# Block 2's norms: the shift from two tiles, the order of the sums, who centres, and the order of three FFN products

## The chip, the cores and the metric

One core of a Trainium2 chip runs the whole program. Times are device microseconds of one execution. TensorE multiplies, VectorE (DVE), ScalarE (ACT) and GpSimd (POOL) work elementwise, SyncE (SP) issues the loads.

## The reference, cut to what matters

Two different transformer blocks follow each other, each with two layers, over 512 tokens and 1024 model columns in float32. The change touches block 2 alone. Each of its layers is

```python
mix = hybrid_mixer(x, ...)
x = layer_norm(ALPHA * x + mix, ln1_g, ln1_b)
cross = memory_cross_attention(x, mem, w_mq, w_mkv, w_mo)
x = layer_norm(ALPHA * x + cross, ln2_g, ln2_b)
ff = squared_relu_mlp(x, w_ff1, w_ff2)      # 1024 -> 4096 -> 1024
x = layer_norm(ALPHA * x + ff, ln3_g, ln3_b)

def layer_norm(x, g, b):
    mu = mean(x); var = mean((x - mu) ** 2)
    return (x - mu) * rsqrt(var + 1e-5) * g + b
```

## The kernel before

Activations lie with the model column on the partitions: x is eight chunks of 128 columns by 512 tokens (`x[:, n, :]`). A product's output tile is 128 columns by 512 tokens and is summed over eight chunks of the input. Every float32 operand is split in two parts of a faster format, `hi` and `lo`, and a product takes three matmuls per chunk: w_hi by x_hi (L511), w_lo by x_hi (L514), w_hi by x_lo (L517). `dense` issues the three of one chunk, `tiles` the chunks of one output tile, or of several side by side. Weights come through three staging buffers; ScalarE writes a weight tile's high part (`split_hi`, L998), VectorE its low part (`split_lo`, L1487), into three buffers, so tile n waits for product n - 3. Results go to four PSUM slots in the fixed order of `rings()`.

Each engine has its own written-out program, and semaphores (`did`, `done`) join them; an instruction waits behind everything ahead of it on its engine. `Banks` keeps who must have read a PSUM bank before TensorE writes it again.

A norm follows the eight output tiles of `w_mix`, `w_mo` or the last part of `w_ff2`: six norms in all. Its mean and variance are sums over partitions, so they are matmuls by a matrix of ones, in float32, which take two passes each. So that E[x^2] - mean^2 stays exact, x is first shifted by the mean of its first half of tiles. The steps:

- Tiles 0 to 3: VectorE adds the product to ALPHA x (`added`, L1750); GpSimd adds up the four (`total`, L2209); after product 4, TensorE sums over partitions (`shift_sum`, L864), and ScalarE copies the negative mean (`shift`, L1350).
- VectorE adds the shift to tiles 0 to 3 (`shifted`, L1964); from tile 4 on it adds it to x ahead of the product (`pre`, L1972) and the product after it (`shifted`, L1968). ScalarE squares each shifted tile (L1345), and GpSimd adds up tiles 0 to 6 (`d_sum`, L2216) and their squares (`sq_sum`, L2211 and L2219), 13 operations.
- `tensor_statistics`: four sums, over `total2` (L873), x of tile 7 (L875), the squares (L877) and the last square (L879). ScalarE copies the mean (L1367) and squares it (L1369); VectorE forms the variance (`ln_var`, L2012), ScalarE the reciprocal root (L1041, L1043), VectorE two Newton steps (L1508, L1510).
- `centred` takes the mean off: tiles 0, 2, 3, 6 on VectorE (L2001), 1, 4, 5, 7 on GpSimd (L2226). VectorE multiplies by the root (`ln_scaled`, L2024), ScalarE applies gain and bias twice, to the next product's high part (L1384) and to x (L1385; the last norm writes x alone, L1380), and the low part of even chunks is VectorE's (L2007), of odd chunks GpSimd's (L2231).

Behind `w_mix` TensorE has other work, the keys of the memory (`w_mk`, one tile ahead of the sums and seven after), and then the queries (`w_mq`). Behind `w_mo` come the tiles of `w_ff1`, the first two side by side, behind `w_ff2` of layer 0 the token-major products of the next layer (`token_major`, L562, L564, L568), and behind the last norm the stores of the output.

## Time and profile before

| | before |
|---|---|
| median of three runs | 3048.58 us (3047.69 to 3049.86) |
| profiled execution | 3042.06 us |
| its span | 3040.2 us |
| TensorE busy | 2858.9 us, 94% |
| VectorE, ScalarE, GpSimd busy | 1643.0, 1260.2, 571.0 us |
| mean granted TensorE clock | 0.977 |

The busy times are those of one profiled execution. Matmuls overlap, so the start of one to the start of the next is the time that it holds the engine. A row ends, in brackets, with the idle time of the engine before it and what ended it.

### The profile page before, as it was taken

How to read it: one execution, taken by the hardware profiler on the slowest of the kernel's cores; microseconds unless marked ns; L12 is line 12 of the kernel's file. 1: busy time of each engine (PE TensorE's matmuls, PEld its weight loads, DVE VectorE, ACT ScalarE, POOL GpSimd, SP SyncE). 2: the span in 40 equal slices, each digit the busy share in tenths (PEclk: the TensorE clock that was granted, in tenths of full speed). 3: DMA queues.
4: the chain of work that ended last, by engine and by line, in shares of the span. 5: the costliest groups of instructions: out<-in, count | busy, mean ns of one | idle time of the engine just before them, and what ended most of it. 6: DMA issues, size and time to landing. Idle time of an engine off the chain costs nothing.

```text
span 3040.2 us, 38912 instructions
## 1 busy us (share of the span) xinstructions
PE 2858.9 (94%) x15604; PEld 2371.1 (78%) x15608; DVE 1643.0 (54%) x2509; ACT 1260.2 (41%) x2104; POOL 571.0 (19%) x435
## 2 busy tenths in 40 slices
PE   8988999999979999999999979999799899799997
PEld 7778999998767888886667758888666678588885
DVE  5785644455875744546846353333558664443334
ACT  5673322234763422225445343333344544343333
POOL 2342000011341000002334140000423342400003
PEclk9999999999989999999999989999899999899998
DMA  4111232232112333231133123332211222122221
GB/s 140 45 43 63 91 92 89 91 98 67 44 36 79 98 97 97 86 105 53 60 101 104 45 66 97 97 97 91 72 62 57 94 98 70 56 85 95 97 94 60
DMA packets 71923, 244.35 MB, mean 80 GB/s; under 512 B 9152, under 2 KB 10816, under 8 KB 71744
## 3 DMA queue, kind: packets, MB, share of 16 engines
q1 hardware_dynamic: 66528, 235.50, 24.1%
q10 hardware_dynamic: 5216, 6.36, 0.6%
q8 instruction: 125, 2.05, 0.3%
q14 instruction: 54, 0.44, 0.0%
HBM read 239.73 MB, written 2.10 MB: 80 GB/s over the span
## 4 chain that ended last, share of the span: by engine, by line
PE 78%; DVE 11%; issue 4%; ACT 4%; POOL 3%; DMA 0%; ACTq 0%; DVEq 0%; POOLq 0%
PE psum L511 21%; PE psum L517 21%; PE psum L514 21%; PE psum L536 2%; PE psum L568 2%; PE psum L562 2%; PE psum L564 1%; DVE temp L1915 1%; DVE weights_hi_lo L1487 1%; DVE small L1913 1%; PE psum L914 1%; PE psum L926 1%; ACT weights_hi_lo L998 1%; PE psum L760 1%; POOL temp L2216 1%
## 5 line engine op out<-in xcount | busy, mean ns | idle before, releaser
L511 PE MATMUL psum<-act_hi_lo,weights_hi_lo 128*128 128x512 f32 (+2 forms) x2640 | 822.0, 349 | 17.5 <-ACT act_hi_lo L1384 15.0
L514 PE MATMUL psum<-act_hi_lo,weights_hi_lo 128*128 128x512 f32 (+2 forms) x2640 | 798.0, 340 | 1.9 <-DVE weights_hi_lo L1487 1.9
L517 PE MATMUL psum<-act_hi_lo,weights_hi_lo 128*128 128x512 f32 (+2 forms) x2640 | 796.6, 339 | 0.3
L1487 DVE TENSOR_TENSOR weights_hi_lo<-weights_float,weights_hi_lo 128x1024 fp32r<-128x1024 f32 (+2 forms) x446 | 572.0, 1283 | 263.5 <-ACT weights_hi_lo L998 262.1
L998 ACT ACTIVATE weights_hi_lo<-weights_float 128x1024 fp32r<-128x1024 f32 (+2 forms) x446 | 463.7, 1041 | 507.8 <-PE psum L517 435.3
L511 PEld LDWEIGHTS psum<-act_hi_lo,weights_hi_lo 128*128 128x128 f32 x2640 | 461.2, 190 | 83.2 <-issue 25.2
L511 PE MATMUL psum<-hidden_hi_lo,weights_hi_lo 128*128 128x512 f32 (+1 forms) x1488 | 501.3, 363 | 12.0 <-ACT hidden_hi_lo L1168 7.3
L517 PEld LDWEIGHTS psum<-act_hi_lo,weights_hi_lo 128*128 128x128 f32 x2640 | 458.5, 189 | 58.8 <-DVE act_hi_lo L2007 1.7
L514 PEld LDWEIGHTS psum<-act_hi_lo,weights_hi_lo 128*128 128x128 f32 x2640 | 459.5, 190 | 57.1 <-issue 3.1
L517 PE MATMUL psum<-hidden_hi_lo,weights_hi_lo 128*128 128x512 f32 (+1 forms) x1488 | 493.1, 358 | 1.7 <-POOL hidden_hi_lo L1744 1.2
L514 PE MATMUL psum<-hidden_hi_lo,weights_hi_lo 128*128 128x512 f32 (+1 forms) x1488 | 492.5, 357 | 0.6 <-DVE weights_hi_lo L1487 0.6
L511 PEld LDWEIGHTS psum<-hidden_hi_lo,weights_hi_lo 128*128 128x128 f32 x1488 | 265.4, 189 | 53.9 <-ACT hidden_hi_lo L1168 8.8
L517 PEld LDWEIGHTS psum<-hidden_hi_lo,weights_hi_lo 128*128 128x128 f32 x1488 | 264.7, 189 | 44.0 <-POOL hidden_hi_lo L1744 2.2
L514 PEld LDWEIGHTS psum<-hidden_hi_lo,weights_hi_lo 128*128 128x128 f32 x1488 | 265.3, 189 | 41.2 <-DVE weights_hi_lo L1487 1.5
L1750 DVE SCALAR_TENSOR_TENSOR x_residual<-x_residual,psum 128x512 f32<-128x512 f32 (+1 forms) x136 | 94.0, 691 | 335.1 <-PE psum L517 335.0
L2071 DVE TENSOR_TENSOR hidden_hi_lo<-temp,hidden_hi_lo 128x512 fp32r<-128x512 f32 x64 | 44.3, 692 | 220.9 <-ACT hidden_hi_lo L1454 220.9
L2176 POOL TENSOR_SCALAR temp<-temp,small 128x512 f32<-128x512 f32 (+3 forms) x96 | 106.4, 1119 | 229.1 <-DVE small L1873 229.1
L2209 POOL TENSOR_TENSOR temp<-x_residual 128x512 f32<-128x512 f32 x6 | 13.3, 2216 | 718.6 <-DVE x_residual L1750 718.6
L2112 POOL TENSOR_TENSOR temp<-temp 128x528 f32<-128x528 f32 (+1 forms) x24 | 34.0, 1417 | 434.4 <-ACT temp L1035 433.7
L1202 ACT ACTIVATE hidden_hi_lo<-temp 128x528 fp32r<-128x528 f32 (+1 forms) x44 | 28.1, 639 | 205.3 <-DVE temp L1786 205.3
L1448 ACT ACTIVATE temp<-psum 128x512 f32<-128x512 f32 x64 | 38.2, 598 | 171.9 <-PE psum L517 171.9
L562 PE MATMUL psum<-weights_hi_lo,act_hi_lo 128*128 128x512 f32 (+1 forms) x208 | 84.6, 407 | 20.9 <-ACT weights_hi_lo L998 9.8
(246 smaller groups left out, 3304.3 us busy)
## 6 DMA issues: line engine op xcount, KB each, us to landing
weights_float<-in_w_ff SPq DMA_DIRECT2D x128, 512.0 KB, 3.5
weights_float<-in_w_gu SPq DMA_DIRECT2D x88, 512.0 KB, 3.4
weights_float<-in_w_in SPq DMA_DIRECT2D x70, 512.0 KB, 3.4
weights_float<-in_w_down SPq DMA_DIRECT2D x32, 448.0 KB, 3.3
weights_float<-in_w_out SPq DMA_DIRECT2D x16, 512.0 KB, 3.4
weights_float<-in_w_down SPq DMA_DIRECT2D x16, 512.0 KB, 3.5
weights_float<-in_w_mv SPq DMA_DIRECT2D x16, 512.0 KB, 3.2
weights_float<-in_w_mix SPq DMA_DIRECT2D x16, 512.0 KB, 3.2
```

Of the source, the lines that this page charges most:

```text
L511: e.matmul(slot[:, place:place + c1 - c0], w_hi[:, col], x_hi[:, c0:c1], start=first, stop=False)
L514: e.matmul(slot[:, place:place + c1 - c0], w_lo[:, col], x_hi[:, c0:c1], start=False, stop=False)
L517: mm = e.matmul(slot[:, place:place + c1 - c0], w_hi[:, col], x_lo[:, c0:c1], start=False, stop=final)
L536: mm = e.matmul(slot[:, place:place + c1 - c0], weights, moving[:, c0:c1], start=first, stop=final)
L562: e.matmul(bank, act[:, 0, here], w_hi[:, wk], start=k == 0, stop=False)
L568: mm = e.matmul(bank, act[:, 1, here], w_hi[:, wk], start=False, stop=k == DC - 1)
L998: e.activation(K.parts(n)[0][:, 0:cols], K.staged(n)[:, 0:cols], ACT.Copy).then_inc(*K.did("hi", n))
L1448: e.activation(tmp, K.bank[2 * RING["w_ff1", l, f]], ACT.Relu).then_inc(*did("relu", l, f))
L1487: e.tensor_tensor(lo[:, 0:cols], K.staged(n)[:, 0:cols], hi[:, 0:cols].bitcast(F32), ALU.subtract).then_inc(*K.did("lo", n))
L1750: e.scalar_tensor_tensor(along(x, width), along(x, width), alpha, across(K.psum[slot], width), ALU.mult, ALU.add).then_inc(*K.did(*mark))
L2071: e.tensor_tensor(lo, K.relu[f % 3][:, 0:T2], hi.bitcast(F32), ALU.subtract).then_inc(*did("hid_lo2", l, f))
L2176: e.tensor_scalar(prob, prob, m["small"][u % 4][:, 6 + c:7 + c], None, ALU.mult).then_inc(*did("scaled", l, u, c))
```

## The change

The shift is taken from two tiles (`SHIFT_TILES = 2`) instead of four, and the sum over partitions for it stands after product 2. In `tensor_statistics` the two sums over finished additions come ahead of the two over tile 7. ScalarE squares the mean straight from PSUM ahead of copying it, and runs a one-column reciprocal root ahead of waiting for the sum. GpSimd's `pool_statistics` is gone: VectorE centres all eight tiles and writes all low parts, with `w_mix` two chunks behind `ln_scaled`, with `w_mo` and `w_ff2` after the last one. The first three tiles of `w_ff1` run side by side, with all their high parts of x first.

```diff
-            keys += [(name, l, n)] + ([("shift", name, l)] if n == DC // 2 else [])
+            keys += [(name, l, n)] + ([("shift", name, l)] if n == SHIFT_TILES else [])
...
-LO_POOL = ("mix1", "mix2", "w_mix", "w_mo", "w_ff2")
+LO_POOL = ("mix1", "mix2")
...
+def dense_high(e, w, K, n, slot, at, x, there, first):
+
+    (w_hi, w_lo), col = K.parts(n), slice(at * P, (at + 1) * P)
+    w.wait_ge(*K.done("hi", n))
+    w.wait_ge(*there[0])
+    e.matmul(slot[:, 0:T2], w_hi[:, col], x[0], start=first, stop=False)
+    w.wait_ge(*K.done("lo", n))
+    e.matmul(slot[:, 0:T2], w_lo[:, col], x[0], start=False, stop=False)
+
+
+def tiles_high_first(e, w, K, B, group, inputs, order):
+
+    for n, slot, by in group:
+        B.clear(2 * slot, 2 * slot + 1)
+    for k in order:
+        for n, slot, by in group:
+            x, there = inputs(k)
+            dense_high(e, w, K, n, K.psum[slot], k, x, there, k == order[0])
+    for n, slot, by in group:
+        w_hi = K.parts(n)[0]
+        for k in order:
+            x, there = inputs(k)
+            w.wait_ge(*there[1])
+            mm = e.matmul(K.psum[slot][:, 0:T2], w_hi[:, k * P:(k + 1) * P], x[1], start=False, stop=k == order[-1])
+        mm.then_inc(*K.did("product", n))
+        B.emptied((2 * slot, 2 * slot + 1), by)
...
-        if n == DC // 2:
+        if n == SHIFT_TILES:
             slot = RING["shift", name, l]
             B.clear(2 * slot)
-            w.wait_ge(*K.done("total", name, l, DC // 2 - 1))
+            w.wait_ge(*K.done("total", name, l, SHIFT_TILES - 1))
...
     w.wait_ge(*K.done("d_sum", name, l, DC - 2))
     e.matmul(K.bank[2 * slot], ones, K.total2[:, 0:T2], start=True, stop=False)
+    w.wait_ge(*K.done("sq_sum", name, l, DC - 2))
+    e.matmul(K.bank[2 * slot + 1], ones, K.squares[:, 0:T2], start=True, stop=False)
     w.wait_ge(*K.done("shifted", name, l, DC - 1))
     e.matmul(K.bank[2 * slot], ones, x[:, DC - 1, :], start=False, stop=True).then_inc(*K.did("mean_sum", name, l))
-    w.wait_ge(*K.done("sq_sum", name, l, DC - 2))
-    e.matmul(K.bank[2 * slot + 1], ones, K.squares[:, 0:T2], start=True, stop=False)
     w.wait_ge(*K.done("ln_square", name, l, DC - 1))
...
-            tiles(e, w, K, B, up[0:2], inputs, list(range(DC)), T2)
-            up = up[2:]
+            tiles_high_first(e, w, K, B, up[0:3], inputs, list(range(DC)))
+            up = up[3:]
...
-    for n in range(half):
+    for n in range(SHIFT_TILES):
         split_hi(e, w, K, PIECE[key(n)] + 3)
     w.wait_ge(*done("shift_sum", name, l))
...
-    split_hi(e, w, K, PIECE[key(half)] + 3)
-    for n in range(half + 1):
+    split_hi(e, w, K, PIECE[key(SHIFT_TILES)] + 3)
+    for n in range(SHIFT_TILES + 1):
         square(n)
-    for n in range(half + 1, DC - 1):
+    for n in range(SHIFT_TILES + 1, DC - 1):
         split_hi(e, w, K, PIECE[key(n)] + 3)
         square(n)
...
+    e.activation(K.m["small"][7][:, 0:1], K.m["ones"][:, 0:1], ACT.Abs_reciprocal_sqrt).then_inc(*did("table", name, l))
     w.wait_ge(*done("mean_sum", name, l))
+    e.activation(square, K.bank[2 * slot], ACT.Square, scale=1.0 / D).then_inc(*did("mean_square", name, l))
     e.activation(mean, K.bank[2 * slot], ACT.Copy, scale=1.0 / D).then_inc(*did("mean", name, l))
-    w.wait_ge(*done("mean", name, l))
-    e.activation(square, mean, ACT.Square).then_inc(*did("mean_square", name, l))
...
-    half = DC // 2
+    half = SHIFT_TILES
...
     def low(k):
-        if out is not None and k >= 0 and k % 2 == 0:
-            hi, lo = out(k, T2)
-            w.wait_ge(*done("ln_out", name, l, k))
-            e.tensor_tensor(lo, x[:, k, :], hi.bitcast(F32), ALU.subtract).then_inc(*did("in_lo", name, l, k))
+        hi, lo = out(k, T2)
+        w.wait_ge(*done("ln_out", name, l, k))
+        e.tensor_tensor(lo, x[:, k, :], hi.bitcast(F32), ALU.subtract).then_inc(*did("in_lo", name, l, k))
...
-    for n in (0, 2, 3):
+    w.wait_ge(*done("mean", name, l))
+    for n in range(3):
         centred(n)
...
     for k in range(DC):
-        if k == 6:
-            centred(6)
         if k >= 3:
+            centred(k)
             w.wait_ge(*done("ln_out", name, l, k - 3))
-        w.wait_ge(*done("centred" if k in (0, 2, 3, 6) else "centred_pool", name, l, k))
+        w.wait_ge(*done("centred", name, l, k))
         e.tensor_tensor(K.tmp_ring[k % 3][:, 0:T2], x[:, k, :], q, ALU.mult).then_inc(*did("ln_scaled", name, l, k))
         keys(k + 2)
-        low(k - 2)
-    low(DC - 2)
+        if out is not None and stage_keys is not None and k >= 2:
+            low(k - 2)
+    if out is not None:
+        for k in range(DC - 2 if stage_keys is not None else 0, DC):
+            low(k)
...
-    for n in range(1, DC // 2):
+    for n in range(1, SHIFT_TILES):
         w.wait_ge(*done("added", name, l, n))
...
-def pool_statistics(e, w, K, l, name, out):
-    x, did, done = K.m["x"][:, :, META:T1], K.did, K.done
-    w.wait_ge(*done("mean", name, l))
-    for n in (1, 4, 5, 7):
-        e.tensor_tensor(x[:, n, :], x[:, n, :], K.total2[:, 0:T2], ALU.subtract).then_inc(*did("centred_pool", name, l, n))
-    if out is not None:
-        for k in range(1, DC, 2):
-            hi, lo = out(k, T2)
-            w.wait_ge(*done("ln_out", name, l, k))
-            e.tensor_tensor(lo, x[:, k, :], hi.bitcast(F32), ALU.subtract).then_inc(*did("in_lo_pool", name, l, k))
```

## Rows read from the trace of the kernel before

**Rows 1.** the page, the chain that ended last: share of the span by engine.
```profile
PE 78%; DVE 11%; issue 4%; ACT 4%; POOL 3%; DMA 0%; ACTq 0%; DVEq 0%; POOLq 0%
```

**Rows 2.** who waited for whom, TensorE: us in total, times, longest.
```profile
PE psum L873 <- POOL temp L2216: 39.3, 6, 7.9
```

**Rows 3.** TensorE's timeline, norm behind w_mo, layer 0: start, duration, instructions [idle before].
```profile
1761.09 1.02 PE L864 MATMUL psum<-temp,ones 128*128 128x512 f32 x2
...
1778.21 0.39 PE L517 MATMUL psum<-act_hi_lo,weights_hi_lo 128*128 128x512 f32 x1
1786.53 2.04 PE L873 MATMUL psum<-temp,ones 128*128 128x512 f32 x2 [7.93 <-POOL temp L2216]
...
1791.78 1.28 PE L879 MATMUL psum<-temp,ones 128*128 128x512 f32 x2
1800.56 0.77 PE L511 MATMUL psum<-act_hi_lo,weights_hi_lo 128*128 128x512 f32 x1 [7.50 <-ACT act_hi_lo L1384]
```

**Rows 4.** one-microsecond stretches, TensorE, same norm: length, busy (times), clock, DMA.
```profile
1782.00:1783.00 1.00, 0.00 (x0) 0.53 0.00 0
...
1805.00:1806.00 1.00, 1.00 (x4) 0.52 0.00 0
```

**Rows 5.** GpSimd and VectorE: timeline rows; by line min/median/max ns, first and last start.
```profile
1766.92 1.80 POOL L2211 TENSOR_SCALAR temp<-temp 128x512 f32<-128x512 f32 x1 [9.14 <-ACT temp L1345]
...
L2216 POOL TENSOR_TENSOR temp<-temp,x_residual x30: 1257/1524/2285, 1609.5 to 3017.4; 128x512 f32<-128x512 f32 x30
...
L1972 DVE SCALAR_TENSOR_TENSOR x_residual<-x_residual,temp x24: 678/884/1789, 1600.9 to 3008.9; 128x512 f32<-128x512 f32 x24
...
2982.55 2.21 POOL L2209 TENSOR_TENSOR temp<-x_residual 128x512 f32<-128x512 f32 x1 [312.49 <-DVE x_residual L1750]
...
2985.61 0.69 DVE L1750 SCALAR_TENSOR_TENSOR x_residual<-x_residual,psum 128x512 f32<-128x512 f32 x1 [2.01 <-PE psum L517]
```

**Rows 6.** TensorE's timeline, norm behind w_ff2, layer 0, and the products that follow.
```profile
2156.07 0.39 PE L517 MATMUL psum<-hidden_hi_lo,weights_hi_lo 128*128 128x512 f32 x1
...
2168.64 1.02 PE L879 MATMUL psum<-temp,ones 128*128 128x512 f32 x2
2178.08 0.72 PE L562 MATMUL psum<-weights_hi_lo,act_hi_lo 128*128 128x456 f32 x1 [8.42 <-ACT act_hi_lo L1384]
...
2179.42 0.75 PE L568 MATMUL psum<-weights_hi_lo,act_hi_lo 128*128 128x456 f32 x1 [0.24 <-DVE act_hi_lo L2007]
...
2201.88 0.37 PE L568 MATMUL psum<-weights_hi_lo,act_hi_lo 128*128 128x456 f32 x1
```

**Rows 7.** timeline, norm behind w_mix, layer 0: TensorE's first and last sum, ScalarE.
```profile
1624.73 2.04 PE L873 MATMUL psum<-temp,ones 128*128 128x512 f32 x2 [5.28 <-POOL temp L2216]
...
1629.23 1.02 PE L879 MATMUL psum<-temp,ones 128*128 128x512 f32 x2
...
1661.64 1.28 ACT L1420 ACTIVATE arena<-psum 128x512 f32<-128x512 f32 x2 [2.36 <-PE psum L517]
```

**Rows 8.** timeline, last norm: TensorE's first and last sum, VectorE, ScalarE.
```profile
3018.78 2.04 PE L873 MATMUL psum<-temp,ones 128*128 128x512 f32 x2 [5.13 <-POOL temp L2216]
...
3024.03 1.27 PE L879 MATMUL psum<-temp,ones 128*128 128x512 f32 x2
...
3031.13 3.70 DVE L2024 TENSOR_TENSOR temp<-x_residual,temp 128x512 f32<-128x512 f32 x6
...
3031.86 5.92 ACT L1380 ACTIVATE x_residual<-temp,params 128x512 f32<-128x512 f32 x8 [4.44 <-DVE temp L2024]
```

**Rows 9.** ScalarE's timeline, norm behind w_mo, layer 0, and the third FFN product's use.
```profile
1791.59 1.28 ACT L1041 ACT_TABLE_LOAD   x1
...
1820.20 0.60 ACT L1448 ACTIVATE temp<-psum 128x512 f32<-128x512 f32 x1 [0.54 <-PE psum L517]
```

**Rows 10.** VectorE's timeline, norm behind w_mo, layer 0: centring and Newton's first step.
```profile
1793.78 3.74 DVE L2001 TENSOR_TENSOR x_residual<-x_residual,temp 128x512 f32<-128x512 f32 x3
1797.44 0.68 DVE L1508 SCALAR_TENSOR_TENSOR temp<-temp 128x512 f32<-128x512 f32 x1
```

More of the change, by code:

```diff
@@ L317 @@
     W_FREE1[chain] = [] if before is None else [("normed" if before[0] == "qk" else "sub_scaled", *before[1:])]
+SHIFT_TILES = 2
 def rings():
@@ L853, in tile @@
     def tile(n):
-        by = ("added", name, l, n) if n < DC // 2 else ("shifted", name, l, n)
+        by = ("added", name, l, n) if n < SHIFT_TILES else ("shifted", name, l, n)
         return (PIECE[key(n)], RING[name, l, n], by)
@@ L873, in tensor_statistics @@
     e.matmul(K.bank[2 * slot], ones, K.total2[:, 0:T2], start=True, stop=False)
+    w.wait_ge(*K.done("sq_sum", name, l, DC - 2))
+    e.matmul(K.bank[2 * slot + 1], ones, K.squares[:, 0:T2], start=True, stop=False)
     w.wait_ge(*K.done("shifted", name, l, DC - 1))
     e.matmul(K.bank[2 * slot], ones, x[:, DC - 1, :], start=False, stop=True).then_inc(*K.did("mean_sum", name, l))
-    w.wait_ge(*K.done("sq_sum", name, l, DC - 2))
-    e.matmul(K.bank[2 * slot + 1], ones, K.squares[:, 0:T2], start=True, stop=False)
     w.wait_ge(*K.done("ln_square", name, l, DC - 1))
     e.matmul(K.bank[2 * slot + 1], ones, K.last_sq[:, 0:T2], start=False, stop=True).then_inc(*K.did("sq_stat", name, l))
-    B.emptied((2 * slot,), ("mean", name, l))
+    B.emptied((2 * slot,), ("mean", name, l), ("mean_square", name, l))
     B.emptied((2 * slot + 1,), ("ln_var", name, l))
@@ L1345, in square @@
         e.activation(sq[:, 0:T2], x[:, n, :], ACT.Square).then_inc(*did("ln_square", name, l, n))
-    for n in range(half):
+    for n in range(SHIFT_TILES):
         split_hi(e, w, K, PIECE[key(n)] + 3)
     w.wait_ge(*done("shift_sum", name, l))
-    e.activation(K.total[:, 0:T2], K.bank[2 * RING["shift", name, l]], ACT.Copy, scale=-1.0 / (half * P)).then_inc(
+    e.activation(K.total[:, 0:T2], K.bank[2 * RING["shift", name, l]], ACT.Copy, scale=-1.0 / (SHIFT_TILES * P)).then_inc(
         *did("shift", name, l))
-    split_hi(e, w, K, PIECE[key(half)] + 3)
-    for n in range(half + 1):
+    split_hi(e, w, K, PIECE[key(SHIFT_TILES)] + 3)
+    for n in range(SHIFT_TILES + 1):
         square(n)
-    for n in range(half + 1, DC - 1):
+    for n in range(SHIFT_TILES + 1, DC - 1):
         split_hi(e, w, K, PIECE[key(n)] + 3)
@@ L1958, in vector_normed @@
     x, did, done = K.m["x"][:, :, META:T1], K.did, K.done
-    half = DC // 2
+    half = SHIFT_TILES
     def shifted(n):
@@ L2237, in pool_block2 @@
     pool_normed(e, w, K, l, "w_mix")
-    pool_statistics(e, w, K, l, "w_mix", K.hid_chunk)
     for s in range(STEPSX):
@@ L2245, in pool_block2 @@
     pool_normed(e, w, K, l, "w_mo")
-    pool_statistics(e, w, K, l, "w_mo", K.act_chunk)
     pool_normed(e, w, K, l, "w_ff2")
-    pool_statistics(e, w, K, l, "w_ff2", K.act_chunk if l + 1 < DEPTH else None)
 def pool_program(e, K):
```

## The prediction

> **What bounds the kernel now.** I read the page's chain of waits first: TensorE carries 78% of the chain that ended last, VectorE 11%, GpSimd 3% [rows 1]. So only stretches in which TensorE is idle, or runs at its lower clock, can give time back. The list of who waited for whom says where: the largest single wait of TensorE is at L873, the first matmul of a norm's sums in block 2, for GpSimd's additions at L2216: 39.3 us in six waits, one per norm (block 2 has two layers with three norms each) [rows 2]. Then I read one norm closely, the one behind `w_mo` of layer 0, engine by engine; the same norm in layer 1 has the same durations 856.7 us later.
>
> There the last product's last matmul starts at 1778.21, so TensorE is free at about 1778.45. Its first sum starts at 1786.53, after 7.93 us of idleness [rows 3]. By then its clock is at the half level: the granted clock fell to 0.50 (1.2 GHz) at about 1782, 3.5 us after the last product [rows 4]. So the four sums take 6.55 us, up to the end of L879 at 1793.06, where such a sum at the full clock (2.4 GHz) takes 1.02 from start to end at L864, of which 0.15 lies beside the next matmul: 0.87 [rows 3]. TensorE then idles again for 7.50 us until the first normed chunk. The reader is to see in GpSimd's rows that its chain starts at 1766.92, 5.83 us after the shift matmul (1761.09), and ends `d_sum` 6 just before L873 starts, 19.5 us later, whatever TensorE does [rows 3, 5].
>
> **The change, part by part.** E is the end of a norm's last product, and the sums below are per norm.
>
> *Shift after two tiles.* The shift matmul moves from behind product 4 to behind product 2, that is 2 x 5.44 = 10.9 us earlier; it needs only one addition of GpSimd (2.21 us [rows 5]), which is done some 0.8 us before product 2 ends (2982.55 + 2.21 against 2985.6, where the product's result is added [rows 5]). GpSimd still has 13 operations. Started 5.83 us behind that matmul's start and at the old pace it would end `d_sum` 6 25.3 us after it; product 7 ends 0.9 + 5 x 5.44 = 28.1 us after it. The other bound is product 6 itself: its end at 22.6, `shifted` 0.7, one slow addition 2.28: 25.7, and `sq_sum` 6 by 27.4. So the wait of 39.3 us goes, with 2.4 us to spare.
>
> *Sums that are there added first.* What is late next is `shifted` 7 (E + 0.7) and its square (E + 1.4). The two sums over `total2` and `squares` cover these: 2 x 0.87 us. So four sums follow E without a gap and at the full clock, and `sq_stat` is there at E + 3.65 (4 x 0.87, and 0.15 for the last one's end). In `w_mix` the key product w_mk 0 stands between, which puts it at 1622.95. Gains at `sq_stat`: w_mo 1793.1 - 1782.1 = 11.0; w_ff2 of layer 0 2169.65 - 2159.95 = 9.7; the last norm 3025.3 - 3017.15 = 8.15; w_mix 1630.25 - 1622.95 = 7.3 [rows 3, 6 to 8]. The E of the last norm is 3018.78 - 5.13 - 0.16 = 3013.5; in w_mix TensorE is free at 1624.73 - 5.28 - 0.15 = 1619.3.
>
> *ScalarE's table load and square.* The load takes 1.28 us and stands in w_mix and w_mo, not in w_ff2 [rows 9]. In w_mo it was hidden behind the sums; now ScalarE squares chunk 7 and splits a weight tile until E + 2.5, loads until E + 3.8, runs a one-column operation that no row shows (between nothing and the 0.60 of a full one; I take 0.2), and `mean_square` is ready at E + 4.6. That is 0.95 us behind `sq_stat`: the load turns from hidden to a cost of 0.95 in w_mo. In w_mix the load no longer stands behind key 1 (1.28 gained, but not on TensorE's path); in w_ff2 nothing. `mean_square` straight from PSUM costs 0.60, as L1448 does [rows 9].
>
> *VectorE alone.* `centred` three times took 3.74 us beside GpSimd; alone such an operation takes 0.61 (six of L2024 in 3.70), so 1.9: 1.8 us gained [rows 8, 10]. VectorE takes over 4 `centred` and 4 `low` per norm, 0.61 each, 44 in all, 26.8 us. `centred` k and `ln_scaled` k depend on each other, as Newton's two steps, whose first takes 0.68 and hands over after 0.71 [rows 10], so 1.35 per chunk; ScalarE's output takes 0.74 at the end [rows 8] and 0.70 in w_mo, so 1.41 per chunk where there are two of them, which hides VectorE.
>
> *w_mo, both layers.* `ln_var` at E + 5.3, `centred` to 7.3, Newton 1.45, first scaled chunk E + 9.4, ScalarE's first high part starts at 1787.95 in place of 1799.60 and TensorE at 1788.9 instead of 1800.56 [rows 3]: 11.65 gained. TensorE restarts at 1.2 GHz, as before: 5.35 us until 1805.9 [rows 4], in which 12.4 matmuls fit at 0.43, then 0.232 each. It has 48 high matmuls, six per 1.41 us of arrivals, so it is the bound itself: 1788.9 + 5.35 + 35.6 x 0.232 = 1802.5. All low parts are written by 1800.7. 24 low matmuls end at 1808.05; before, the third product was taken up at 1820.20 [rows 9], so ended at 1820.1. High parts first thus give only 0.4 beyond the start, since TensorE was filled in both. Against it: the fourth tile's weights are split only after product 0, which now ends late (1804.4); hi 2.9 later, lo 1.25 later, 1808.7: 0.5 us of stall. Net 11.6 each.
>
> *w_ff2 of layer 0.* The high part of chunk 0 comes at 2164.8 instead of 2177.12 (TensorE starts on it at 2178.08 [rows 6]): 12.3 gained. But now all low parts stand behind the last `ln_scaled`, and the token-major products that follow take their terms in the order high, high, low. Low part 0 is there 8.5 us behind the start of the first high part's writing, before it was 2.3 [rows 6]. TensorE does two matmuls and waits until 2173.3, then 94 of them, 14 at half clock in 5.35 us and 80 at 0.206: 2195.1, before 2202.1. Gained 6.9; 5.4 of the 12.3 are given back.
>
> *w_mix, both layers.* TensorE was nearly full from `sq_stat` on (keys, then w_mq 0 and 1, taken up at 1661.64 [rows 7]; idle for some 0.5 in between). VectorE now needs 1.35 + 1.14 + 0.61 = 3.1 us per chunk, ScalarE 2.65. Followed, Newton ends at 1630.2 (before 1638.5), the keys end at 1643.1, w_mq 1's low part comes at 1643.6, low part 5 at 1650.9, 0.4 to 0.9 of stalls in all, and w_mq 0 and 1 end at 1655.1 instead of 1661.6: 6.4 of the 7.3.
>
> *The last norm.* Newton ends at 3021.4 instead of 3031.1. Then VectorE is the bound, with five chunks at 1.35 in place of ScalarE's eight at 0.74 [rows 8]: the last chunk is scaled at 3030.0, written at 3030.85, and the stores take the same 2.4 us after it. Before it was written at 3037.78. Gained 7.0.
>
> Sum: 2 x 6.4 + 2 x 11.6 + 6.9 + 7.0 = 49.9 us. The profiled execution took 3042.06 us (span 3040.2), which becomes 2992.2; the median of the runs shown is 3048.58, 6.5 above it, and I carry the saving over unchanged: **2998.7**.
>
> **The shared port, weighed.** In rows, `pre` (L1972) takes 0.68 at least and 1.79 at most, and GpSimd's addition 1.26 or 2.28 [rows 5]. My pace above has such meetings in it. The Trainium skill, SBUF — State Buffer, "Who interferes with whom", says that a VectorE instruction with two SBUF inputs and a GpSimd one that reads SBUF exclude each other for the whole instruction; the trace's 1.79 and 2.28, near the sum of the two short ones, agree.
>
> **Rivals.**
> 1. *GpSimd stays late.* If every product's stretch held 2 additions of 1.27 and two VectorE operations with two SBUF inputs (0.68, 1.14) one after the other, 4.4 of 5.44 us, the backlog of seven us shrinks by 1.0 per tile only: `d_sum` 6 at about 29.1 and `sq_sum` 6 at 30.4 against 28.1 and 29.0, 1.4 late in four norms: 3004. That serial order is what the Trainium skill's rule above gives. With all 13 operations at 2.28 the wait would stay nearly whole and only the later parts gain, up to 3030. For it: the slow rows. Against: the old chain met the same operations and took 19.5. 15%.
> 2. *The clock stays up.* If TensorE's idle stretches, now once per norm and shorter (5.7 to 7 us), left the clock at 2.4 GHz, each of three restarts would gain about 2.5: 2991. Against: it fell 3.5 us after the last product [rows 4]. 8%.
> 3. *VectorE becomes the bound: slower.* Place: from `sq_stat` to the first products. Price: its 26.8 us moved, all on the path, and 6.2 for low part 0, while the sums gain nothing since the 13 additions still end last: 3048.6 + 33 = 3082, or any part of it. It decides once the sums come less than about 5.5 us earlier per norm. Against: 1.41 of ScalarE per chunk hides 1.35. 3%.
> 4. *No effect*, since something else ends the wait at L873 (`shifted`, banks): the rows name L2216 in all six. 2%.
>
> My forecast has 72%. Unknown costs move it by about 1.5 us per norm, so 2990 to 3008 for itself; with rival 1 I give 2988 to 3012. A difference of 0.2% (6 us) can be told from none. Faster 94%, within 0.2% 3%, slower 3%.
>
> **What would show it.** After: no wait of L873 for L2216; the four sums 0.9 apart behind the last product at a granted clock of 1.00; `sq_stat` at E + 3.7; three `centred` in 1.9; a wait of some 6.5 us at L568 for the low part on VectorE in layer 0's w_ff2; VectorE ahead of ScalarE at the very end. Wrong would be a wait of the sums for GpSimd, or a first high part less than 10 us earlier in w_mo.

## The result, and the profile after

| | before | after |
|---|---|---|
| median | 3048.14 us (3044.42 to 3049.86, 4 runs) | 2990.68 us (2987.5 to 2993.9, 4 runs) |
| profiled execution | 3042.06 us | 2990.75 us |
| its span | 3040.2 us | 2988.9 us |
| mean granted TensorE clock | 0.977 | 0.984 |

The ratio is 0.982 (95% interval 0.9807 to 0.9832): 57.5 us faster by the medians, 51.3 by the two profiled executions. Forecast were 49.9 us and 2998.7 us; the time lies in the range of 2988 to 3012.

The changed kernel has other line numbers. TensorE: the shift matmul L896, the four sums L906 to L912 (before L873 to L879), the first high matmul of `w_ff1` L531, the token-major three L594, L596 and L600. GpSimd: its chain starts at L2246, its additions are L2251 and L2254. ScalarE: the square of a tile L1377, `mean_square` L1401, the high part L1417. VectorE: `pre` L2005, `shifted` L2001, `ln_var` L2044, `centred` L2034, Newton L1541 and L1543, `ln_scaled` L2056, the low part L2039.

First, who waited for whom on TensorE (total us, times, longest), to set against [rows 2]:

```profile
PE psum L531 <- ACT act_hi_lo L1417: 13.1, 2, 6.5
...
PE psum L600 <- DVE act_hi_lo L2039: 6.8, 1, 6.8
...
PE psum L594 <- ACT act_hi_lo L1417: 5.6, 1, 5.6
```

The 39.3 us in six waits are gone. Left is the wait for the first high part, in the three norms where a product needs it next (both `w_mo`, `w_ff2` of layer 0), and there is a new one of 6.8 us at L600, that for the low part in `w_ff2` of layer 0.

TensorE's timeline of the norm behind `w_mo` of layer 0 (start, duration, [idle before]), to set against [rows 3]; then its stretches of two microseconds (length, busy, granted clock, DMA share, GB/s):

```profile
1742.90 1.02 PE L896 MATMUL psum<-temp,ones 128*128 128x512 f32 x2
...
1771.01 0.40 PE L521 MATMUL psum<-act_hi_lo,weights_hi_lo 128*128 128x512 f32 x1
1771.24 1.02 PE L906 MATMUL psum<-temp,ones 128*128 128x512 f32 x2
1772.10 1.02 PE L908 MATMUL psum<-temp,ones 128*128 128x512 f32 x2
1772.96 1.02 PE L910 MATMUL psum<-x_residual,ones 128*128 128x512 f32 x2
1773.82 1.02 PE L912 MATMUL psum<-temp,ones 128*128 128x512 f32 x2
1781.38 0.77 PE L531 MATMUL psum<-act_hi_lo,weights_hi_lo 128*128 128x512 f32 x1 [6.54 <-ACT act_hi_lo L1417]
```

```profile
1774.00:1776.00 2.00, 0.84 (x2) 1.00 0.00 0
1776.00:1778.00 2.00, 0.00 (x0) 1.00 0.78 262
1778.00:1780.00 2.00, 0.00 (x0) 0.64 0.00 0
1780.00:1782.00 2.00, 0.62 (x2) 0.50 0.00 0
1782.00:1784.00 2.00, 2.00 (x6) 0.50 0.00 0
1784.00:1786.00 2.00, 2.00 (x7) 0.65 0.01 4
```

The four sums follow the last product 0.86 us apart at a clock of 1.00. With E = 1771.24 the first high matmul stands at E + 10.14; before it was E + 22.1. The clock falls after the sums, in the idle stretch, and the products restart at half.

VectorE in the same norm, against [rows 10], and the end of GpSimd's additions, against [rows 5]:

```profile
1775.84 0.69 DVE L2044 SCALAR_TENSOR_TENSOR temp<-psum,temp 128x512 f32<-128x512 f32 x1 [0.77 <-ACT temp L1401]
1776.45 1.88 DVE L2034 TENSOR_TENSOR x_residual<-x_residual,temp 128x512 f32<-128x512 f32 x3
1778.25 0.68 DVE L1541 SCALAR_TENSOR_TENSOR temp<-temp 128x512 f32<-128x512 f32 x1
```

```profile
1748.73 1.81 POOL L2246 TENSOR_SCALAR temp<-temp 128x512 f32<-128x512 f32 x1 [6.63 <-ACT temp L1377]
...
1767.44 2.27 POOL L2251 TENSOR_TENSOR temp<-temp,x_residual 128x512 f32<-128x512 f32 x1
1769.67 1.74 POOL L2254 TENSOR_TENSOR temp<-temp 128x512 f32<-128x512 f32 x1
```

The 13 operations end at 1771.41, and the sum over squares wants the last of them at 1772.10: on time, by 0.7 us. The sum over x wants the twelfth, done at 1769.71, at 1771.24: by 1.5 us.

A stage is measured best from one norm's E to the next, since that leaves out how late the execution was when it came there. In us, for the profiled executions (before and e1, where the first sum waits: its start, less its idle time and 0.16; "last norm" goes to the end of the span):

```
                        mix-mo    mo-ff2    ff2-mix   mix-mo    mo-ff2    last    sum
                        layer 0   layer 0   0 to 1    layer 1   layer 1   norm
before                  159.2     377.9     319.8     159.1     378.3     26.7   1420.9
after                   153.0     366.0     313.6     151.8     366.6     19.7   1370.7
after (e0_after_again)  151.4     366.1     312.0     151.6     365.6     19.7   1366.5
after (e11_after_third) 151.4     366.2     313.8     151.4     366.5     19.7   1369.1
e1_shift_four           158.9     375.9     324.3     159.4     375.3     27.9   1421.9
e8_shift_two_only       151.7     368.6     311.9     151.7     368.7     19.7   1372.3
e6_pairs_low_late       153.0     372.3     312.2     151.4     372.5     19.7   1381.2
e4_low_near_ff2         153.4     365.8     307.3     151.5     366.1     19.7   1363.8
e2_old_order            151.5     366.2     313.8     151.5     366.5     20.0   1369.3
e3_gpsimd_shares        152.9     370.6     311.9     152.8     369.5     20.7   1378.3
e5_pairs_low_near       151.5     367.2     307.0     151.7     367.2     19.7   1364.2
e7_table_early          151.6     365.7     312.3     151.5     365.7     19.7   1366.4
e9_near_and_table       151.4     365.3     307.8     151.9     364.3     19.7   1360.4
e10_warm                151.4     363.0     307.0     151.9     363.4     19.7   1356.3
```

Three executions of the changed kernel differ by up to 1.8 us in a stage, mostly where the clock dips, that is, stands at half for a few microseconds while TensorE is busy, in one and not in another (in `after`, ff2-mix and the first mix-mo have such a dip). Differences below that are told from the rows of the norm itself.

### The profile page after: what moved, and what is told of

Read it like the earlier page. It is cut to its first block, busy times and chain, and to the rows that moved or that the text cites. A ratio compares the mean times of both kernels' runs of the same rounds, so it can differ in the third digit from the quotient of the medians.

```text
span 2988.9 us, 38922 instructions
## 1 busy us (share of the span) xinstructions
PE 2844.5 (95%) x15604; PEld 2367.5 (79%) x15608; DVE 1651.0 (55%) x2553; ACT 1257.4 (42%) x2110; POOL 503.6 (17%) x379
## 4 chain that ended last, share of the span: by engine, by line
PE 82%; DVE 12%; ACT 3%; POOL 1%; issue 1%; DMA 0%; ACTq 0%; DVEq 0%
PE psum L515 22%; PE psum L521 22%; PE psum L518 22%; PE psum L568 2%; PE psum L600 2%; PE psum L594 2%; PE psum L596 2%; DVE weights_hi_lo L1520 1%; DVE temp L1948 1%; PE psum L947 1%; DVE small L1946 1%; PE psum L959 1%; PE psum L792 1%; PE psum L800 1%; DVE temp L2056 1%
## 5 line engine op out<-in xcount | busy, mean ns | idle before, releaser
L515 PE MATMUL psum<-act_hi_lo,weights_hi_lo 128*128 128x512 f32 (+2 forms) x2592 | 800.7, 347 | 2.5 <-ACT temp L1132 1.6
L518 PE MATMUL psum<-act_hi_lo,weights_hi_lo 128*128 128x512 f32 (+2 forms) x2592 | 777.2, 338 | 2.6 <-DVE weights_hi_lo L1520 2.6
L521 PE MATMUL psum<-act_hi_lo,weights_hi_lo 128*128 128x512 f32 (+2 forms) x2592 | 775.5, 337 | 0.0
L515 PEld LDWEIGHTS psum<-act_hi_lo,weights_hi_lo 128*128 128x128 f32 x2592 | 450.6, 190 | 64.4 <-issue 8.3
L518 PEld LDWEIGHTS psum<-act_hi_lo,weights_hi_lo 128*128 128x128 f32 x2592 | 449.1, 189 | 56.2 <-DVE weights_hi_lo L1520 4.0
L521 PEld LDWEIGHTS psum<-act_hi_lo,weights_hi_lo 128*128 128x128 f32 x2592 | 448.3, 189 | 54.0
L1783 DVE SCALAR_TENSOR_TENSOR x_residual<-x_residual,psum 128x512 f32<-128x512 f32 (+1 forms) x124 | 85.6, 690 | 312.9 <-PE psum L521 312.8
L1235 ACT ACTIVATE hidden_hi_lo<-temp 128x528 fp32r<-128x528 f32 (+1 forms) x44 | 28.1, 639 | 204.5 <-DVE temp L1819 204.5
L594 PE MATMUL psum<-weights_hi_lo,act_hi_lo 128*128 128x512 f32 (+1 forms) x208 | 84.4, 406 | 18.3 <-ACT weights_hi_lo L1031 10.0
```

What stands on the lines that cost most here:

```text
L515: e.matmul(slot[:, place:place + c1 - c0], w_hi[:, col], x_hi[:, c0:c1], start=first, stop=False)
L518: e.matmul(slot[:, place:place + c1 - c0], w_lo[:, col], x_hi[:, c0:c1], start=False, stop=False)
L521: mm = e.matmul(slot[:, place:place + c1 - c0], w_hi[:, col], x_lo[:, c0:c1], start=False, stop=final)
L594: e.matmul(bank, act[:, 0, here], w_hi[:, wk], start=k == 0, stop=False)
L1783: e.scalar_tensor_tensor(along(x, width), along(x, width), alpha, across(K.psum[slot], width), ALU.mult, ALU.add).then_inc(*K.did(*mark))
```

## The experiments

They ran in three groups, each on one chip with runs of the kernel before (e1, e8, e6 and e4; e2, e3 and e5; e7, e9 and e10). The first group has no runs of the changed kernel, so its times are set beside those of other groups, and their ratios to before decide. The two others held the changed kernel once more, as their measure, with nothing edited:

> The changed kernel once more, as the measure for the other three on the same chip: 2990.5 (2988 to 2994).

> The changed kernel as the measure for the other three on the same chip: 2990 (2987.5 to 2993.5).

Measured: 2989.08 us (2987.61 to 2992.85), ratio 0.9813 (0.9798 to 0.9828), and 2990.99 us (2987.49 to 2993.52), ratio 0.9811 (0.9798 to 0.9825), both as expected.

### What brings the saving: the shift

**e1_shift_four** keeps all of the change but the shift.

```diff
-SHIFT_TILES = 2
+SHIFT_TILES = 4
```

> The changed kernel with the shift from four tiles again, all else as changed. Theory (the saving is the earlier sums): by the terms at sq_stat, 2 x 7.3 + 2 x 11.0 + 9.7 + 8.15 = 54.4 us come back, so about 3043 us (3036 to 3049), no better than the kernel before by more than 8 us; the trace shows TensorE waiting at the first sum for GpSimd, some 39 us over six norms, and the clock at half in the sums. Rival (most comes from the order of the sums, VectorE alone and the high parts first): only some 20 us come back, 3010 us.

Measured: 3048.13 us, ratio 1.0002 (0.9993 to 1.0011). The waits of its TensorE and the timeline at `w_mo` of layer 0:

```profile
PE psum L906 <- POOL temp L2251: 38.7, 6, 7.8
```

```profile
1786.67 2.04 PE L906 MATMUL psum<-temp,ones 128*128 128x512 f32 x2 [7.67 <-POOL temp L2251]
```

The old wait is back, and with it the half clock (2.04 us for a sum). All the rest of the change together is worth nothing while GpSimd's additions end last. By the stages that is a sum of gains and losses: each mo-ff2 is 2.0 to 3.0 us shorter than before, but ff2-mix is 4.5 longer, with the wait of 6.76 us at L600 in it, and the last norm 1.2.

**e8_shift_two_only** is the other side: the kernel before, with the shift after two tiles and nothing else.

```diff
-            keys += [(name, l, n)] + ([("shift", name, l)] if n == DC // 2 else [])
+            keys += [(name, l, n)] + ([("shift", name, l)] if n == SHIFT_TILES else [])
...
-    half = DC // 2
+    half = SHIFT_TILES
```

> The kernel before with nothing but the shift from two tiles. Theory: the sums gain their 54.4 us here too, and by my own terms the other parts together are worth 2 x 0.6 in w_mo, -2.8 in w_ff2 of layer 0, -1.15 at the end and about 0 in w_mix, so this is about 2.5 us faster than the whole change: 2988 us (2984 to 2992). Rival (each part helps): 5 to 10 us slower than the whole change, 2996 to 3001, since centring beside GpSimd costs 1.8 us in each norm.

Measured: 2997.12 us (2994.41 to 2999.12), ratio 0.9837 (0.9822 to 0.9852). The time is the rival's: the shift alone brings 48 to 50 us. The remainder, worth 0 without it, adds something on top: 6 us by the medians, on different chips and with ratios whose intervals touch (0.9822 to 0.9852, 0.9807 to 0.9832), and 1.6 to 5.8 us by the stages. Those of mix-mo and of the last norm are as long here as in the changed kernel: their gain is the shift's alone. What the remainder gains stands in mo-ff2, 2.1 to 3.1 us each; ff2-mix gives 0.1 to 1.9 of it back. VectorE, GpSimd and TensorE of this kernel at `w_mo` of layer 0 (E = 1776.51) show why the sum behind my expectation missed it:

```profile
1781.08 4.27 DVE L2004 TENSOR_TENSOR x_residual<-x_residual,temp 128x512 f32<-128x512 f32 x3
1785.27 1.75 DVE L1511 SCALAR_TENSOR_TENSOR temp<-temp 128x512 f32<-128x512 f32 x1
```

```profile
1779.64 6.83 POOL L2229 TENSOR_TENSOR x_residual<-x_residual,temp 128x512 f32<-128x512 f32 x4 [3.26 <-ACT temp L1370]
```

```profile
1789.45 0.76 PE L514 MATMUL psum<-act_hi_lo,weights_hi_lo 128*128 128x512 f32 x1 [9.09 <-ACT act_hi_lo L1387]
```

GpSimd centres four tiles from 1779.64 to 1786.47, and meanwhile VectorE's three centrings take 4.27 us in place of 1.88 and the first Newton step 1.75 in place of 0.68. The first high matmul stands at E + 12.94, against E + 10.14.

### GpSimd's share of the norm

**e3_gpsimd_shares** gives GpSimd its centrings and odd low parts back, inside the changed kernel.

```diff
+def pool_statistics(e, w, K, l, name, out):
+    x, did, done = K.m["x"][:, :, META:T1], K.did, K.done
+    w.wait_ge(*done("mean", name, l))
+    for n in (1, 4, 5, 7):
+        e.tensor_tensor(x[:, n, :], x[:, n, :], K.total2[:, 0:T2], ALU.subtract).then_inc(*did("centred_pool", name, l, n))
...
-    for n in range(3):
+    for n in (0, 2, 3):
         centred(n)
```

> GpSimd gets its share of the norm back (centring of chunks 1, 4, 5, 7 and the odd low parts, as before the change); the shift after two tiles, the order of the sums, mean_square from PSUM and high parts first stay. Theory A (GpSimd's four centrings block VectorE's centring and its Newton steps): three `centred` take 4.2 in place of 1.9 and the first Newton step about 1.7 in place of 0.7, the first high part comes 2.5 to 3 us later per norm: +2.8 in each w_mo, +2 in each w_mix, about -3 in w_ff2 of layer 0 (the wait of L600 for the low part falls from 6.8 to about 0), about 0 in the last norm: 2997 (2994 to 3000). Theory B (the prediction's own terms, 1.8 for the centring and nothing else): +1.8 in each w_mo, +1 in each w_mix, -5 in w_ff2, -1 in the last norm: 2990 (2988 to 2992).

Measured: 3000.59 us (2999.28 to 3002.51) beside 2989.08 (2987.61 to 2992.85) for the changed kernel in the same group: 11.5 us slower. Theory B, the term of my prediction, is out; theory A has the mechanism and still priced it too low. The same place (E = 1773.70), VectorE, GpSimd and TensorE:

```profile
1778.91 5.07 DVE L2034 TENSOR_TENSOR x_residual<-x_residual,temp 128x512 f32<-128x512 f32 x3
1783.90 1.75 DVE L1541 SCALAR_TENSOR_TENSOR temp<-temp 128x512 f32<-128x512 f32 x1
```

```profile
1778.83 6.27 POOL L2260 TENSOR_TENSOR x_residual<-x_residual,temp 128x512 f32<-128x512 f32 x4 [5.26 <-ACT temp L1402]
```

```profile
1788.09 0.76 PE L531 MATMUL psum<-act_hi_lo,weights_hi_lo 128*128 128x512 f32 x1 [10.80 <-ACT act_hi_lo L1417]
```

The first high matmul stands at E + 14.39 instead of E + 10.14, so 4.25 us per norm: 5.07 for three centrings (3.2 more) and a Newton step blocked for 1.1. In e8 it stood at E + 12.94, 1.45 earlier, and the rows give two parts. VectorE's first centring starts at E + 5.21 here and at E + 4.57 there (0.64), since the changed ScalarE program stands behind the table load. And the mean is handed over 5.1 us behind E, where in e8 it was there at E + 3.1: GpSimd starts at the same moment as VectorE, and the three centrings take 5.07 in place of 4.27 (0.8). The stages say the same: mo-ff2 2.9 to 4.6 longer, mix-mo 1.4, last norm 1.0, and ff2-mix no longer, since the low parts there are near. So the edits of the change are no separate gains: beside GpSimd's share, ScalarE's new order costs in these rows. That order was not undone by itself.

### Order of the sums and of ScalarE's work

**e2_old_order** puts the middle two sums back.

```diff
-    w.wait_ge(*K.done("sq_sum", name, l, DC - 2))
-    e.matmul(K.bank[2 * slot + 1], ones, K.squares[:, 0:T2], start=True, stop=False)
     w.wait_ge(*K.done("shifted", name, l, DC - 1))
     e.matmul(K.bank[2 * slot], ones, x[:, DC - 1, :], start=False, stop=True).then_inc(*K.did("mean_sum", name, l))
+    w.wait_ge(*K.done("sq_sum", name, l, DC - 2))
+    e.matmul(K.bank[2 * slot + 1], ones, K.squares[:, 0:T2], start=True, stop=False)
```

> The order of the two middle sums put back: the sum over x[7] ahead of the sum over squares. Theory (what is late behind the last product is `shifted` 7, and one sum in front of it covers it almost): in w_mo of layer 0 `shifted` 7 was ready about 0.96 us behind E and would be wanted at E + 0.86, so the sums lose 0.1 us per norm; mean_sum is there one sum (0.86) earlier, which gives back up to 0.86 where ScalarE's chain (table load, mean_square) was late, but its table load stands behind the square of chunk 7 and not behind the sum, so nothing of that is gained: 2990.5 to 2991, the same. Rival (the order is worth something: GpSimd's sq_sum 6 is only 0.7 us ahead of its use, so a later use of it saves waits; ScalarE's mean_square starts earlier in w_ff2 and the last norm, where no table load stands): 0.3 to 0.8 us faster per norm in three norms, 2988.5 to 2989.5. Rival 2 (the prediction's reason for the edit: the uncovered square costs 0.7 per norm): 2995.

Measured: 2992.12 us (2989.54 to 2995.09) beside 2989.08 for the changed kernel in the group; the intervals of the ratios overlap (0.9807 to 0.9838, 0.9798 to 0.9828). Its sums at `w_mo` of layer 0:

```profile
1772.41 1.02 PE L906 MATMUL psum<-temp,ones 128*128 128x512 f32 x2
1773.42 1.12 PE L908 MATMUL psum<-x_residual,ones 128*128 128x512 f32 x2
```

L908, now the sum over tile 7, starts 1.01 us behind L906 instead of 0.86: one sum covers all but 0.15 us of `shifted` 7, and the last sum starts at E + 2.83 instead of 2.57. The first high matmul is at E + 10.14 all the same:

```profile
1782.55 0.76 PE L531 MATMUL psum<-act_hi_lo,weights_hi_lo 128*128 128x512 f32 x1 [6.28 <-ACT act_hi_lo L1417]
```

So in the rows the order is worth nothing in both `w_mo` and, where no table load stands, 0.26 in `w_ff2` of layer 0 (first product at E + 9.50 against E + 9.24) and 0.3 in the last norm; the 3.0 of the medians I can't place, and the sum of its stages (1369.3) lies beside those of the changed kernel (1366.5 to 1370.7).

**e7_table_early** takes the table load off the path.

```diff
+    e.activation(K.m["small"][7][:, 0:1], K.m["ones"][:, 0:1], ACT.Abs_reciprocal_sqrt).then_inc(*did("table", name, l))
     square(DC - 1)
     split_hi(e, w, K, PIECE[key(DC - 1)] + 3)
...
-    e.activation(K.m["small"][7][:, 0:1], K.m["ones"][:, 0:1], ACT.Abs_reciprocal_sqrt).then_inc(*did("table", name, l))
     w.wait_ge(*done("mean_sum", name, l))
```

> ScalarE's load of the root table moved ahead of the square of the last chunk, where the engine stood idle for 4.7 us. Theory (behind the last product the load is on the path: mean_square of w_mo in layer 0 starts 3.99 us behind E, and sum x[7] is done 2.7 us behind E): mean_square then starts behind the weight split, at about E + 2.9, ln_var follows sq_stat at E + 3.65 instead of starting at E + 4.6, so 0.9 us per norm in the two w_mo; in w_mix the load is not last, 0; w_ff2 has none. From one first sum to the next: w_mo to w_ff2 365.2 in place of 366.1; whole kernel 1.8 faster: 2988.2 on the median, 2986 to 2991. Rival (squares or copies bring the other table back, so that the load stands twice): 1.3 to 2.6 us slower, 2992.

Measured: 2990.76 us (2988.95 to 2993.52) beside 2990.99 (2987.49 to 2993.52) for the changed kernel in the group. In its timeline (E = 1773.18) the load is done before the square; ScalarE, then TensorE:

```profile
1769.46 1.28 ACT L1390 ACT_TABLE_LOAD   x1
...
1775.95 0.60 ACT L1401 ACTIVATE temp<-psum 128x512 f32<-128x512 f32 x1 [0.21 <-PE psum L910]
```

```profile
1782.44 0.77 PE L531 MATMUL psum<-act_hi_lo,weights_hi_lo 128*128 128x512 f32 x1 [5.67 <-ACT act_hi_lo L1417]
```

The first high matmul is at E + 9.26, 0.88 us earlier, as the 0.95 of the prediction had it; mo-ff2 took 365.7 in both layers, against 365.6 to 366.6. The medians don't show 1.8 us: too small for them. No table is loaded more often than in the changed kernel.

### Low parts and high parts

**e4_low_near_ff2** writes the low parts of `w_ff2` in layer 0 two chunks behind `ln_scaled`, as in `w_mix`.

```diff
+def NEAR(name, stage_keys):
+    return stage_keys is not None or name == "w_ff2"
...
-        if out is not None and stage_keys is not None and k >= 2:
+        if out is not None and NEAR(name, stage_keys) and k >= 2:
             low(k - 2)
```

> The changed kernel, but in w_ff2 of layer 0 the low parts stand two chunks behind ln_scaled, as in w_mix. Theory: the wait for low part 0 (6.8 us at L600) shrinks to about 1 and TensorE starts in earnest 5.5 us earlier; VectorE then needs 1.95 us per chunk, less than the 2.5 us that TensorE needs per chunk: 5 to 5.5 us faster, 2985.4 us. Rival (the wait only moves on to a later chunk's high part, since VectorE becomes slower than ScalarE): under 2 us faster.

Measured: 2985.24 us (2983.95 to 2989.56), ratio 0.9801 (0.9786 to 0.9816), where 2985.4 was expected. In place of the 6.76 us at L600 its token-major products wait 0.24 and 0.42:

```profile
2149.39 0.75 PE L604 MATMUL psum<-weights_hi_lo,act_hi_lo 128*128 128x456 f32 x1 [0.24 <-DVE act_hi_lo L2043]
...
2151.32 0.75 PE L604 MATMUL psum<-weights_hi_lo,act_hi_lo 128*128 128x456 f32 x1 [0.42 <-DVE act_hi_lo L2043]
```

ff2-mix, 312.0 to 313.8 us in the changed kernel, falls to 307.3. The change gives this away.

**e6_pairs_low_late** undoes high parts first and leaves the low parts late.

```diff
-            tiles_high_first(e, w, K, B, up[0:3], inputs, list(range(DC)))
-            up = up[3:]
+            tiles(e, w, K, B, up[0:2], inputs, list(range(DC)), T2)
+            up = up[2:]
```

> The changed kernel with the first w_ff1 tiles in one pair again, with high, high, low in turn, while the low parts stay behind the last ln_scaled. Theory: TensorE waits for low part 0, which is there 7.8 us behind the first matmul; third product about 36.1 us behind the last w_mo product in place of 28.7: 7.4 us slower in each layer, 3005.5 us (3002 to 3009). Rival (TensorE's half clock is the bound either way): under 4 us slower in all.

Measured: 3007.95 us (3002.49 to 3009.72), ratio 0.9875 (0.9859 to 0.9892). A wait like that of L600, once per `w_mo`, where high parts first had the high matmuls to fill it:

```profile
PE psum L521 <- DVE act_hi_lo L2039: 13.3, 2, 6.7
```

mo-ff2 is 6.2 us longer in layer 0 and 5.9 to 6.9 in layer 1. That is 12 to 13 us; the medians say 17 to 19, and the profiled execution, 3002.49 us, was the fastest of the four, so some 5 us of the median stand in no trace. Late low parts need high parts first.

**e5_pairs_low_near** has neither: pairs as in e6, and `NEAR` true for all norms.

> High parts first undone (the first FFN products of w_mo in a pair, high, low weight and low part per chunk, as before), with every low part written two chunks behind its scaled one, also in w_ff2 of layer 0; VectorE alone. Theory (high parts first is worth nothing by itself; it only pays for low parts that are written late): w_mo +0.4 - 0.5, so as the changed kernel, and w_ff2 gains the 5.3 that the near low part brought by itself: 2985.3 (2983 to 2988). Rival (high parts first hides VectorE's low parts, which otherwise hold up the chunks: 1.35 + 0.61 = 1.96 per chunk against ScalarE's 1.41 where VectorE writes all of them): 8 x 0.55 = 4.4 us later at the last chunk of each w_mo, 2990 to 2994.

Measured: 2989.63 us (2988.62 to 2990.44) beside 2989.08. The median is nearer to the rival, and its mechanism is in the rows, at a lower price than it had. Each chunk costs VectorE 0.69 for its low part as well: in `w_mo` of layer 0 the pairs come 1.93 us apart where ScalarE could do 1.41 (VectorE's rows of e5):

```profile
1792.43 0.68 DVE L2043 TENSOR_TENSOR act_hi_lo<-x_residual,act_hi_lo 128x512 fp32r<-128x512 f32 x1
...
1794.36 0.69 DVE L2043 TENSOR_TENSOR act_hi_lo<-x_residual,act_hi_lo 128x512 fp32r<-128x512 f32 x1
```

By the stages pairs cost 1.1 to 1.5 us per `w_mo` beside e4, not the 4.4 of the rival, and ff2-mix has e4's gain. That should leave it 2 to 6 us ahead of the changed kernel. The profiled execution came late out of block 1 (last section); why the medians show no gain stays open.

### A version that beats both

**e9_near_and_table** is e4 and e7 together. **e10_warm** adds to e9 matmuls on a weight tile, whose results nobody reads, while TensorE would wait for the first high part, in both `w_mo` and in `w_ff2` of layer 0.

```diff
+WARM = 24
+
+def warm(e, w, K, B, n, *banks):
+    w_hi = K.parts(n)[0]
+    B.clear(*banks)
+    w.wait_ge(*K.done("hi", n))
+    for i in range(WARM):
+        e.matmul(K.bank[banks[0]], w_hi[:, 0:P], w_hi[:, 0:BANK], start=True, stop=True)
...
     tensor_statistics(e, w, K, B, l, "w_mo")
+    first = RING["w_ff1", l, 0]
+    warm(e, w, K, B, PIECE["w_ff1", l, 0], 2 * first, 2 * first + 1)
...
             tensor_statistics(e, w, K, B, l, "w_ff2")
+            if l + 1 < DEPTH:
+                warm(e, w, K, B, PIECE["w_tok", l + 1, 0], 4)
```

> Low parts of w_ff2 in layer 0 two chunks behind, and the table load ahead of the last square. Theory: the two gains add up, 4.9 + 1.8 us: 2983.3 (2981 to 2986). Rival (ScalarE's table move costs what it gains): 2985 as without it.

> As the kernel before this one in the job, and TensorE fills its idleness between a norm's sums and the first high part with 24 matmuls of a weight tile on itself (128x512, about 0.23 us each, 5.5 us), into the bank that the next product then starts afresh; in both w_mo and in w_ff2 of layer 0; their results are not used. Theory (the half clock behind each restart, 3.98 us in w_mo and some 7 us with its clock half in w_ff2, comes only from the idle 6.5 and 5.7 us before it): the clock stays at 1.00, the products start full and become bound by ScalarE's 1.41 us per chunk in w_mo (gain 1.8 each) and by VectorE's 1.93 per chunk in w_ff2 (gain 1 to 3): 5.5 us less, 2977.8 (2975 to 2981). Rival A (the clock falls after the sums whatever TensorE does, or later at another place, as it dips in block 1 while busy): 2983, the same as without. Rival B (the fillers end late and hold the first product back): up to 1 us per norm, 2983 to 2986.

Measured, in one group with the changed kernel (2990.99): e9 2985.15 us (2981.3 to 2985.34), ratio 0.979 (0.9777 to 0.9803); e10 2980.0 us (2977.62 to 2982.84), ratio 0.9775 (0.9762 to 0.9788). e10 is the fastest kernel here, 69 us below before. For e9 the median is that of the rival (2985, as without the table move), but the rows show both gains: first high matmul at E + 9.3 in both `w_mo`, ff2-mix at 307.8 us, and stages that sum to 3.4 us less than e4's and 6.1 to 10.3 less than those of the changed kernel. The timeline and clock of e10 at `w_mo` of layer 0:

```profile
1778.19 1.02 PE L916 MATMUL psum<-temp,ones 128*128 128x512 f32 x2
1778.64 6.04 PE L985 MATMUL psum<-weights_hi_lo 128*128 128x512 f32 x24
1784.80 0.50 PE L535 MATMUL psum<-act_hi_lo,weights_hi_lo 128*128 128x512 f32 x1
```

```profile
1782.00:1786.00 4.00, 3.88 (x17) 1.00 0.03 11
1786.00:1790.00 4.00, 4.00 (x18) 1.00 0.01 2
```

The clock stays at 1.00 and the first high matmul (E + 9.19) is not held back, so the half clock there comes from the idle stretch before it, as the theory had it. mo-ff2 gains 2.3 and 0.9. In `w_ff2` the clock stays up too, but VectorE's 1.93 us per chunk is then the bound:

```profile
2149.19 0.47 PE L604 MATMUL psum<-weights_hi_lo,act_hi_lo 128*128 128x456 f32 x1 [0.76 <-DVE act_hi_lo L2059]
2151.12 0.47 PE L604 MATMUL psum<-weights_hi_lo,act_hi_lo 128*128 128x456 f32 x1 [1.05 <-DVE act_hi_lo L2059]
```

so that only 0.8 of the 1 to 3 us came.

## Why the prediction was right, and where it was off

- *Shift.* Right. The additions started at 1748.73, 5.83 us behind the shift matmul as taken over from before; product 7 ended 28.3 us behind it (28.1 forecast). Off by the margin: `d_sum` 6 ended 26.8 us behind the shift matmul, not 25.3 to 25.7, so 1.5 us was spare, not 2.4, and `sq_sum` 6 at 28.5, not 27.4, with 0.7 spare. In two norms L908 waited 0.5 us in all for `sq_sum`: all that came of rival 1.
- *Sums.* Right: 0.86 apart, `sq_stat` at E + 3.6 (3.65 forecast). That they are at the full clock is the shift's doing (e1), hardly the new order's (e2: 0 to 0.3 us per norm). The prediction did not separate the two.
- *Table load.* Right: 0.95 forecast, 0.88 by e7. The one-column operation took 0.20, the value taken.
- *VectorE alone.* The mechanism was right, the size not: 1.8 us per norm for the centring, where giving GpSimd its share back costs 4.25 up to the first high matmul (e3), and 2.8 where the sums and ScalarE have their old order too (e8). The term took GpSimd's interference from where it stood before [rows 10], and not the Newton step that the earlier mean exposes to it. The forecast was not hurt, since it worked out the changed kernel's path directly with unhindered durations: ScalarE's first high part at E + 9.5 forecast (1787.95 less 1778.45), E + 9.18 measured.
- *w_mo.* 11.6 forecast, 11.9 and 11.7 measured. The half clock lasted 3.98 us after the restart in layer 0 and some 5.5 in layer 1, where 5.35 was taken; the fourth tile stalled 0.34 (0.5). The 0.4 given to high parts first beside GpSimd's low parts was not tried by itself.
- *w_ff2, layer 0.* 6.9 forecast, 6.2 measured with a clock dip in the stage, and 6.0 to 7.8 over three executions. The wait for low part 0 was 6.76; the 5.4 given back are the 4.7 to 6.5 us by which e4's stage is shorter.
- *w_mix.* 6.4 forecast; 6.2 and 7.3 measured, the former with a clock dip, 7.5 to 7.8 in the two other executions. The stalls followed, which took 0.9 of the 7.3, cost nothing: TensorE stalled twice for 0.27 us for a low part, in both layers, and before it had stalled for 0.31 and 0.23. Mis-sized by about 1.
- *Last norm.* 7.0 forecast, 7.05 measured; pairs of VectorE 1.40 apart against 1.35:

```profile
2983.59 0.69 DVE L2056 TENSOR_TENSOR temp<-x_residual,temp 128x512 f32<-128x512 f32 x1
2984.19 0.68 DVE L2034 TENSOR_TENSOR x_residual<-x_residual,temp 128x512 f32<-128x512 f32 x1
2984.98 0.69 DVE L2056 TENSOR_TENSOR temp<-x_residual,temp 128x512 f32<-128x512 f32 x1
```

- *The base.* The stages sum to 50.2 us against 49.9 forecast (51.3 with the 1.06 of block 1, which the change doesn't touch). That they agree to 0.3 is partly luck: the same stages sum to 54.4 and 51.8 us in the two other executions of the changed kernel. The 8 us between forecast and median come from carrying the saving to a median 6.5 us above the profiled execution: after the change the profiled execution lay on its median. Where a slower execution of the kernel before spends these 6.5 us no trace shows; only this one was traced.
- *Rivals.* 2, the clock staying up, did not happen by itself: 0.64 at 1778 to 1780, as shown above. e10 makes it happen. 3 needed the sums to stay late, and they came 11 us earlier. 4 is refuted by the result, since the wait at the first sum went and the time fell by 57 us; in e1 both are back.

## What to carry to other kernels

Where one engine's chain ends last at every stage, move its start, and expect the other edits to be worth something else with it than without it (here 2 to 6 us and 0): test the change by undoing each part as well as by doing each alone, and read the gains and losses stage by stage, since a sum of 0 can hide both. Two engines that share work at the critical step can cost more than one that does it all; look at the durations of the same instruction with and without the neighbour, and at what will be beside it once things move. A low part may be late only if there is other work ahead of it, and an idle stretch ahead of a full product can be filled so that the clock stays up.
